# Five 2 MB loads of expert weights issued as nine transfers each, by every eighth row

## The reference, cut to what matters

```python
def moe_ffn(h, router_w, router_b, w_gate_up, b_gate_up, w_down, b_down):
    ...
    for e in range(N_EXPERTS):
        gu = ht @ w_gate_up[e] + b_gate_up[e]
        gate, up = gu[:, :D_FF], gu[:, D_FF:]
        gate = jnp.minimum(gate, SWIGLU_LIMIT)
        up = jnp.clip(up, -SWIGLU_LIMIT, SWIGLU_LIMIT)
        act = gate * jax.nn.sigmoid(SWIGLU_ALPHA * gate) * (up + 1.0)
        out = out + combine[:, e:e + 1] * (act @ w_down[e] + b_down[e])
```

## Time and profile before

| | us |
|---|---|
| median of 3 runs (lowest to highest) | 1238.31 (1237.26 to 1238.64) |
| the profiled execution | 1237.29 |
| its span, first to last instruction | 1235.4 |
| PE busy | 1160.8 (94%) |
| DVE busy | 420.2 (34%) |
| ACT busy | 266.9 (22%) |

### The profile page before, as it was taken

The page is one execution under the profiler, slowest core; times in us unless marked ns, Lnnn a source line. Parts: engine busy times, 40 slices in busy tenths (PEclk is TensorE's granted clock), DMA queues, the critical chain, the costliest instruction groups (busy, mean ns, idle before and its releaser), DMA issues.

```text
span 1235.4 us, 13704 instructions
## 1 busy us (share of the span) xinstructions
PE 1160.8 (94%) x5828; PEld 599.6 (49%) x5828; DVE 420.2 (34%) x703; ACT 266.9 (22%) x422; POOL 0.2 (0%) x4
## 2 busy tenths in 40 slices
PE   7999999999999999999999889888988898889987
PEld 6899968888533443443343324333433333333332
DVE  6777878756421221222112112111221121111112
ACT  6866546344210000010010001000100010000002
POOL 0000000000000000000000000000000000000000
PEclk9999999999999999999999999999999999999999
DMA  9454425698999999999999999999999999999996
GB/s 322 147 157 151 148 91 171 217 399 340 365 425 428 427 428 428 427 429 425 429 426 429 428 428 428 427 428 428 427 428 425 429 427 429 427 429 427 427 426 263
DMA packets 67292, 455.25 MB, mean 368 GB/s; under 512 B 6970, under 2 KB 23771, under 8 KB 39966
## 3 DMA queue, kind: packets, MB, share of 16 engines
q1 hardware_dynamic: 65654, 454.06, 89.8%
q10 hardware_dynamic: 1576, 0.29, 0.1%
HBM read 453.29 MB, written 1.05 MB: 368 GB/s over the span
## 4 chain that ended last, share of the span: by engine, by line
PE 64%; DMA 32%; DVE 2%; issue 1%; ACT 1%; DVEq 0%; ACTq 0%
DMA ring<-in_w_gate_up 28%; PE bank L1201 18%; PE bank L1219 12%; PE total L902 6%; PE bank L902 5%; PE total L890 4%; PE bank L890 4%; DMA ring<-in_w_down 3%; PE bank L960 2%; PE bank L1187 2%; PE bank L979 1%; PE total L1233 1%; PE total L1201 1%; PE bank L1208 1%; PE total L950 1%
## 5 line engine op out<-in xcount | busy, mean ns | idle before, releaser
L1201 PE MATMUL bank<-ring,hy_area 128*64 128x512 f32 x1984 | 444.6, 595 | 43.2 <-DMA ring<-in_w_gate_up 43.2
L1201 PEld LDWEIGHTS bank<-ring,hy_area 128*64 128x64 f32 x1984 | 136.8, 137 | 331.4 <-issue 244.6
L1219 PE MATMUL bank<-ring,xn_area 128*64 128x512 f32 x992 | 220.1, 595 | 0.3 <-DMA ring<-in_w_down 0.3
L2119 DVE TENSOR_SCALAR qk_area<-bank 128x512 f32<-128x512 f32 x31 | 21.4, 692 | 361.3 <-PE bank L1201 361.3
L1219 PEld LDWEIGHTS bank<-ring,xn_area 128*64 128x64 f32 x992 | 68.4, 137 | 134.6 <-issue 122.8
L1682 ACT ACTIVATE qk_area<-qk_area 128x512 f32<-128x512 f32 x32 | 20.2, 630 | 456.7 <-DVE qk_area L2119 456.7
L2130 DVE SCALAR_TENSOR_TENSOR xn_area_r<-bank,tmp_area,xn_area_r 128x512 fp32r<-128x512 f32 x31 | 23.3, 751 | 200.5 <-ACT xn_area_r L1693 200.5
L1823 DVE TENSOR_TENSOR front_r<-ring,slot_r 128x1024 fp32r<-128x1024 f32 x60 | 73.1, 1222 | 22.2 <-ACT slot_r L1493 22.2
L1493 ACT CAST slot_r<-ring 128x1024 fp32r<-128x1024 f32 x60 | 62.8, 1049 | 43.5 <-PE bank L902 23.2
L1693 ACT ACTIVATE xn_area_r<-bank,tmp_area 128x512 fp32r<-128x512 f32 x31 | 21.3, 687 | 234.9 <-PE bank L1219 221.0
L979 PE MATMUL bank<-tmp_area_r 128*128 128x512 f32 x124 | 38.0, 426 | 12.8 <-issue 8.6
(11 more groups left out here) (397 smaller groups left out, 1253.2 us busy)
## 6 DMA issues: line engine op xcount, KB each, us to landing
ring<-in_w_gate_up SPq DMA_DIRECT2D x116, 2048.0 KB, 37.0
ring<-in_w_down SPq DMA_DIRECT2D x54, 2048.0 KB, 38.9
ring<-in_w_in SPq DMA_DIRECT2D x31, 1024.0 KB, 5.7
ring<-in_w_gate_up SPq DMA_DIRECT2D x22, 1024.0 KB, 9.4
ring<-in_w_down SPq DMA_DIRECT2D x19, 1024.0 KB, 9.9
ring<-in_w_branch_gla SPq DMA_DIRECT2D x4, 1024.0 KB, 5.2
ring<-in_w_branch_hy SPq DMA_DIRECT2D x4, 1024.0 KB, 7.7
ring<-in_w_out SPq DMA_DIRECT2D x4, 1024.0 KB, 6.3
```

The lines of the kernel that those rows point to most:

```text
L1201: last = pe.matmul(to[bk][half * CAP:(half + 1) * CAP, :], xeT[:, j, q, :], where(j, c), start=False, stop=(j == GU_CH - 1), skip_group_ch ...
L1219: last = pe.matmul(banks[to][half * CAP:(half + 1) * CAP, :], half_of(turned, f), where(j, c * D + half * 512), start=(f == 0), stop=(f == ...
L2119: nc.vector.tensor_scalar(gate, made[0][:, :], LIMIT, None, ALU.min).then_inc(gate_ready, 1)
```

## The change

Five of the 170 pair loads are no longer issued as one transfer of 128 rows (a row is what goes to one partition, 16 KB), but as nine: seven transfers of 16 rows each, rows r, r+8, r+16 and so on up to r+120 for r from 0 to 6, and then two transfers of 8 rows, rows 7, 15, up to 63, and rows 71, 79, up to 127. Together they carry the same 128 rows into the same places. All nine raise the same semaphore, and TensorE waits for 144 in place of 16.

```diff
+STRIDE = 8
+SPLIT = tuple(n for n, width in LOADS if width == 2)[8::34]
+
+
+def row_parts(n):
+
+    if n not in SPLIT:
+        return [slice(0, P)]
+    return [slice(r, P, STRIDE) for r in range(STRIDE - 1)] + [slice(h + STRIDE - 1, h + P // 2, STRIDE) for h in (0, P // 2)]
+
+
 def expert_arrivals():
...
-        count[s] += 16
+        count[s] += 16 * len(row_parts(n))
...
             def moe(n, width=1):
 
                 s = slot_of(n)
-                sp.dma_start(ring[:, s * SLOT:(s + width) * SLOT], rows_of(*CHUNK_ORDER[n], width)).then_inc(moe_loaded[s], 16)
+                src = rows_of(*CHUNK_ORDER[n], width)
+                for rows in row_parts(n):
+                    sp.dma_start(ring[rows, s * SLOT:(s + width) * SLOT], src[rows, :]).then_inc(moe_loaded[s], 16)
```

## The result

The changed kernel takes 1288.04 us (median of 4 runs, 1281.12 to 1293.82), against 1238.04 us for the kernel before (median of 4, 1237.26 to 1238.64). The ratio is 1.0403, 95% interval 1.0375 to 1.043, which is 46.4 to 53.2 us. Forecast were 1270 us and a range up to 1288. The direction and the collisions came out; the size is 50.0 us in place of 31.8 and lies on the range's upper end. The four runs lie 12.7 us apart, those of before 1.4 us. The profiled execution is the slowest of the four (1293.82 us, span 1292.0), so the sums on its rows are made against its own span, 56.6 us longer than before.

What follows compares the result with a forecast made beforehand. DMA, never idle from 330 to 1215 us, was taken to bound the kernel. Five split loads at 6.35 us each added 31.8 to 1237.3, giving 1269.1; with runs' median 1.0 higher, 1270 us, range 1250 to 1288.

Steps and rivals of the forecast that it cites:

- the sum: Per split load, 9 turns x 0.613 x 2.04 = 11.25 us in place of 4.90; 6.35 more, 31.8 for five.
- rival 4: Engines out of step collide in normal loads too, or short transfers pause: 30 us on top, 1300 us; chance 0.04.
- What bounds the kernel: DMA works without pause from 330 to 1215 us, so each microsecond added there moves the end by a microsecond.
- Issue on SP: Nine issues of 328 ns take 3.0 us per split load, covered by at least 7 us of queued work: no cost.
- The engines' turns: Both 8-row transfers use the same eight engines: nine turns for these, 0.613 us more a load, 3.1 for five.
- The factor of 2.04: Split rows collide entering on-chip memory, slowed 428 / 210 = 2.04 as in the 64-partition `hy_ffn_w3` stretch; bounds 1.71 to 2.46.
- (1) turns only: Rows eight apart have ways of their own, so split loads cost only turns: 3.1 us, 1241.4 us; chance 0.09.
- (2) not slower: A row's partition chooses its engine, so split loads keep eight rows per engine: no change, 1238.3 us; chance 0.05.
- (3): First two splits hidden since PE does not wait on DMA before 640 us: 19 us, 1257 us; chance 0.02.

Runs made afterwards that it cites:

- The kernel by columns: The same five loads cut into eight transfers of 128 partitions with 2 KB each, against the kernel before: 1240.09 us, 2.5 over.
- sixteen transfers: Only pair load 8 split, into 16 transfers of eight rows lying four apart, against the kernel before: 1245.52 us, 7.7 over.
- the engines nearly in step (0.9 us): Queue drained ahead of pair load 141 and load 144 split into nine transfers: 1259.47 us, 7.1 over the kernel with the drain alone.
- eight-transfer kernel: The same five loads split into eight even transfers of 16 rows, every eighth row, against the kernel before: 1279.41 us, 41.8 over.
- A drain: No load split; SP waits ahead of pair load 141 until TensorE has used every loaded chunk, against the kernel before: 1252.34 us, 14.5 over.

## Why the prediction was right in kind and short in size

**The number.** 1288.04 us lies at the very end of the range, and it got there by things that the sum did not hold. By one of the prediction's own signs of being wrong, one split that costs more than 8.7 us, rival 4 came about: the last two dips lost 11.5 and 13.6 us, and load 144 alone cost 10.1.

**What bounds the kernel.** Right. Lost DMA time reaches the end wherever it is lost, at 400 us as well (8.0 us for load 8 alone).

**Issue on SP.** Right that it costs nothing in this change, wrong in its size. The split's issues take 589 ns in the median, not 328:

```profile
L784 SPq DMA_DIRECT2D ring<-in_w_gate_up x11: 328/589/617, 396.8 to 405.9; - x11
```

The next load is issued at 405.9 us in place of 403.8, within the queue's 7 us, and the one behind it at 407.08, as before at 407.24. The kernel by columns, with issues of 0.43 us, bounds issue, completions and shorter packets together at 2.5 us for five. With sixteen transfers the queue did not cover it.

**The engines' turns.** The choice of the same eight engines for both 8-row transfers is shown by the share of 0.58. The Trainium skill (DMA: Bandwidth & Descriptors, on why a DMA increments its semaphore by 16) says so, and the trace agrees that they are always the same; which eight it does not show. One load's ninth turn was priced at 0.613 x 2.04 = 1.25 us and measured 0.7, within what the runs scatter. In the series the difference of the medians is 50.0 - 41.8 = 8.2 us for five, against 6.3 by that price, with intervals that overlap. What is clear is that the uneven turns drive the engines apart: eight of them have 9 rows, eight have 7, and the spread at load 144 is 16.2 us in place of 6.9.

**The factor of 2.04.** It came out: slow packets take 1.16 to 1.24 us, 1.9 to 2.0 times 0.613, where 1.25 was forecast. But the row was not what the prediction took it for. The stretch from 18.4 to 22.4 us is not one of 64-partition transfers alone. Four of five of the data packets that start in its last 1.6 us are the 8 KB ones of `hy_decay`, which goes to all 128 partitions, and they too take twice as long (0.67 us in the median, and 0.31 from 22.5 us on):

```profile
20.80:22.40 1.60, 1.60 (x10) 1.34 (x9) 1.46 (x5) 0.00 (x0) 0.00 (x0) 1.00 1.09 215
```

Why they do is open. The 4 KB packets of `hy_ffn_w3` take 0.40 us from 18.4 to 19.8 us, against 0.16 for those of `dft_table` behind, a factor of 2.5. That the mean of this mixture gave the factor of the split loads is partly luck.

**What the sum left out.** It let only the split load's own 128 rows run at half rate. The runs by every eighth row show 164 to 430 slow packets a split, and the first dip lasts 15 us where some 9 were forecast. With the engines nearly in step (0.9 us) the split lost 5.7 us in the trace, and 7.1 by the medians, which fits the 6.35 of the sum. Load 8 comes at a spread of 2 to 3 us, has 200 slow packets and costs 8.0; for five loads that is 40 in place of 31.8. The other 10 us (50 - 5 x 8.0) come with the larger spreads at the later splits, the last of which has 430. So the term that was mis-sized is the number of rows that collide, not the price of one. Rival 4 named the mechanism ("engines out of step after a split meet in the normal loads as well") and gave it 0.04 and 30 us. It is real, though smaller. They meet only around a split: between the dips the rate is 428 GB/s whatever the spread. With even turns, where the spread at entry is the one of the kernel before, the loss still grows from 6.4 to 9.8 us. So a part of the growth is the drift that was there without the change.

**The profiled execution.** Its dips give 49.4 us of 56.6. In the eight-transfer kernel they give 40.9 of 42.0. The difference fits the end: the last chunk waits for the last engine, and the spread of the last loads is 19.0 us in the one and 8.2 in the other, 7.1 before. A rate over all engines does not show that part.

**The rivals.** (1) turns only, and (2) not slower, both needed a rate above 388 GB/s; it was 205 to 221 in the first dip. (3) fell with load 8 alone. The Trainium skill (SBUF — State Buffer, Door 1), by which rows eight apart lie on eight ports, gives the right order of the forms: every eighth row like 64 neighbours, 16 neighbours dearer. Its half rate for two engines on a port agrees with the 1.9 to 2.0 times of a slow packet; its quarter for 16 neighbours does not show in full, 2.5 times and not 4. No run here separates its rule on p and p + 32 from another map that also puts rows eight apart together.

**Not shown: where the packets collide.** Row r of the source always goes to partition r, so whatever set of rows is moved together, both its source in main memory and its destination on the chip change. The runs show that sets of rows collide, and how much. That it happens on the way into on-chip memory and not on the way out of main memory is argued from the map, which fits; a load that sends other source rows to the same partitions would part the two, and was not tried.

## What to carry to other kernels

Cutting a load by rows is not neutral even where no byte, order or wait changes. What fits all runs here is that the engine goes by a row's place in the transfer and the way by the row itself, and only the load of all 128 rows brings the two together. If a load must be cut, cut it by columns (0.5 us here against 7 to 14). If it is cut by rows, its neighbours in the queue pay as well, so count more than its own packets. And price a disturbance of parallel engines once alone and once in its series, since what it leaves behind may be what the next one costs.

## What the runs showed of the hardware that I had not expected

A collision slows more packets than those of the load that causes it: 164 for a load of 128 with the engines 0.9 us apart, 430 with them 16.2 us apart. Each takes about twice as long, whatever the spread.

The 16 engines drift apart in a queue that is never empty: 2.1 us at 400 us, 7.1 us at 1206 us, with no change made. A drain brings them back to 1.1 us, and costs 14.5 us itself. SP takes 589 ns in the median to issue one of the nine transfers of 16 or 8 rows eight apart, 420 for 16 neighbouring rows and 328 for 128 rows.

PE's granted clock is 1.00 in the stretches between the dips and 0.83 to 0.91 in the four later dips, where PE stood idle for lack of chunks; the mean of a matmul of `gate_up` over the whole span rose from 595 to 608 ns. DMA bounds those stretches, so nothing here says that it cost time.
